# Seven block products in place of eight for twelve of the 22 channel tiles of a down-projection

## The reference

```python
D_MODEL, SEQ, DEPTH, D_FF, CONV_WIDTH = 1024, 512, 2, 2816, 3

def conv_ffn(h, w_up, conv_w, conv_b, w_down):
    gate, val = jnp.split(h @ w_up, 2, axis=-1)
    gate = lax.conv_general_dilated(gate, conv_w[:, None, :], window_strides=(1,),
        padding=((CONV_WIDTH - 1, 0),), dimension_numbers=('NWC', 'WIO', 'NWC'),
        feature_group_count=D_FF) + conv_b
    return (jax.nn.silu(gate) * val) @ w_down
```

## Time and profile before

| what | value |
|---|---|
| median of three runs | 1188.32 us |
| the profiled execution, its own time | 1188.03 us |
| its span | 1186.2 us |
| PE busy | 1174.4 us, 99% |
| granted PE clock, mean | 0.999 of full speed |
| DVE, ACT, POOL busy | 63%, 54%, 57% |
| the two down-projections (from the last up-projection tile to `last_two`) | 498.1 to 596.4 us and 1059.2 to 1157.5 us |

### The profile page before, as it was taken

One profiled execution on the slowest core, in us unless ns is written; L12 is line 12 of the kernel. 1 busy time (PEld: TensorE's weight loads), 2 busy tenths in 40 slices (PEclk: granted clock), 3 DMA queues, 4 the chain that ended last, 5 costly groups with the idle time before them and its releaser, 6 DMA issues.

```text
span 1186.2 us, 21327 instructions
## 1 busy us (share of the span) xinstructions
PE 1174.4 (99%) x7666; PEld 1076.9 (91%) x7670; DVE 746.1 (63%) x1318; ACT 637.3 (54%) x1003; POOL 681.3 (57%) x593
## 2 busy tenths in 40 slices
PE   8999999999999999999999999999999999999997
PEld 7999999889999999988888889978999999998886
DVE  7888777658787777723241375644877787762325
ACT  6665555537665656532343365444766565653334
POOL 2434445326877777666645331611787777766672
PEclk9999999999999999999999999999999999999999
DMA  7232222122332322332223211411233232323221
GB/s 267 100 107 71 90 89 72 36 71 72 115 112 94 110 101 106 125 107 73 104 77 120 106 72 37 142 37 36 75 139 106 98 113 88 113 102 107 92 85 71
DMA packets 17334, 113.83 MB, mean 96 GB/s; under 512 B 1920, under 2 KB 2304, under 8 KB 4608
## 3 DMA queue, kind: packets, MB, share of 16 engines
q1 hardware_dynamic: 16416, 110.20, 26.1%
q10 hardware_dynamic: 864, 2.88, 0.7%
HBM read 110.98 MB, written 2.10 MB: 95 GB/s over the span
## 4 chain that ended last, share of the span: by engine, by line
PE 95%; DVE 2%; ACT 1%; issue 1%; DMA 0%; DVEq 0%; ACTq 0%
PE ps L2118 34%; PE ps L2166 17%; PE ps L1911 9%; PE ps L1768 7%; PE ps L1802 3%; PE ps L1830 3%; PE ps L2299 2%; PE ps L1952 2%; PE ps L1875 2%; PE ps L2279 2%; PE ps L1819 2%; PE ps L1880 1%; PE ps L2203 1%; PE ps L1938 1%; PE ps L1710 1%
## 5 line engine op out<-in xcount | busy, mean ns | idle before, releaser
L350 POOL TENSOR_TENSOR w_lo<-w_raw,w_hi 128x512 fp32r<-128x512 f32 (+2 forms) x169 | 256.9, 1551 | 277.5 <-ACT w_hi L474 221.6
L408 POOL TENSOR_TENSOR w_lo<-w_raw,w_hi 128x512 fp32r<-128x512 f32 x120 | 152.9, 1297 | 85.1 <-ACT w_hi L745 66.6
L474 ACT ACTIVATE w_hi<-w_raw 128x2048 fp32r<-128x2048 f32 (+1 forms) x53 | 95.5, 1801 | 166.4 <-PE ps L2166 129.4
L408 POOL TENSOR_TENSOR s_lo<-s_raw,s_hi 128x512 fp32r<-128x512 f32 x120 | 154.9, 1322 | 0.0
L1454 DVE TENSOR_TENSOR hT_lo<-region,hT_hi 128x2048 fp32r<-128x2048 f32 (+1 forms) x22 | 58.9, 2685 | 138.6 <-ACT hT_hi L821 138.6
L2166 PE MATMUL ps<-w_hi,hT_hi 128*128 128x512 f32 x288 | 112.2, 390 | 0.3
L2166 PE MATMUL ps<-w_hi,hT_lo 128*128 128x512 f32 x288 | 112.0, 389 | 0.0
L2166 PE MATMUL ps<-w_lo,hT_hi 128*128 128x512 f32 x288 | 112.0, 389 | 0.0
L745 ACT ACTIVATE w_hi<-w_raw 128x1536 fp32r<-128x1536 f32 x40 | 59.5, 1488 | 71.8 <-PE ps L2118 71.8
L2118 PE MATMUL ps<-hT_hi,w_hi 128*128 128x256 f32 x320 | 90.8, 284 | 0.0
L2118 PE MATMUL ps<-hT_hi,w_lo 128*128 128x256 f32 x320 | 90.6, 283 | 0.0
(11 more groups left out here) (329 smaller groups left out, 3603.0 us busy)
## 6 DMA issues: line engine op xcount, KB each, us to landing
w_raw<-weights SPq DMA_DIRECT2D x99, 1024.0 KB, 4.8
gain<-gains ACTq DMA_DIRECT2D x4, 512.0 KB, 4.2
x<-x_in SPq DMA_DIRECT2D x3, 512.0 KB, 7.3
out<-region SPq DMA_DIRECT2D x3, 512.0 KB, 2.6
w_raw<-weights SPq DMA_DIRECT2D x2, 384.0 KB, 5.5
w_raw<-weights SPq DMA_DIRECT2D x1, 768.0 KB, 8.5
cst<-consts SPq DMA_DIRECT2D x1, 640.0 KB, 10.3
x<-x_in ACTq DMA_DIRECT2D x1, 512.0 KB, 4.3
```

The lines of the kernel that those rows point to most:

```text
L350: ins = pool.tensor_tensor(w_lo[:, slot, cols], w_raw[:, slot, cols], w_hi[:, slot, cols].bitcast(f32), ALU.subtract)
L408: return pool.tensor_tensor(dst, raw, high.bitcast(f32), ALU.subtract)
L474: sc.activation(w_hi[:, slot, 0:used], w_raw[:, slot, 0:used], ACT.Copy).then_inc(w_hi_ready, 1)
```

## The change

Twelve of the 22 channel tiles are taken as six steps j of two tiles, 2j and 2j+1. In a step the activations are a 2 x 2 of blocks (tokens 0-255 or 256-511 by channel tile 2j or 2j+1: A11, A12, A21, A22) and so are the weights (channel tile by 512 output columns: B11, B12, B21, B22). The products become seven instead of eight, of 6 matmuls each (2 token tiles x 3 passes), with S1 to S4 sums of activation blocks and T1 to T4 sums of weight blocks. They go in three passes over the six steps:

- X units, 0 to 5 after `n1`, one step each: B11, B12 and B22 are loaded (1536 columns). ACT copies B12 to PSUM (`stage_b12`), DVE makes T3 = B22 - B12 and T1 = B12 - B11 (`t1_t3`), ACT the high parts, DVE the low part of T1, POOL those of B11, of S3 and of T3. PE: A11 x B11, S1 x T1, S3 x T3, 18 matmuls a unit.
- Z units, 6 to 8, two steps each, with 2048 columns of plain weights: A12 x B21 and S4 x B22, 24 matmuls a unit. S4 is made by DVE.
- Y units, 9 to 11, two steps each: T3 is copied to PSUM again (`stage_t3`), T2 = T3 + B11 and T4 = T2 - B21 are made by DVE, split by ACT, DVE and POOL. PE: S2 x T2 and A22 x T4, 24 matmuls a unit.

Units 12 to 16 are the other ten channel tiles, 48 matmuls each, as before, with `last_two` on the last two. A layer's down-projection has 17 units in place of 11, and 492 matmuls in place of 528. S1 and S2 are made by POOL during the up-projection (`act_sums`, six pairs). DVE adds the products to `x` in three groups of banks: ten adds after unit 5, four after unit 8 and six after unit 11. The gain of the next norm is loaded by ACT's queue after the X unit 2 and no longer ahead of the down-projection. In `combine_block` of the up-projection the buffer `u2` is now `p1[half]`, in place.

The core of the diff (`down_lows` for the Z and Y units, the Y pass on DVE and the plain units follow the same pattern; a line of "..." is a cut):

```diff
+            for n1, after in ((W_DN0, W_DN1), (W_DN1, W_ALL)):
+                for m in range(n1, n1 + 6):
+                    sp.wait_ge(w_lo_ready, m - 1)
+                    load(m, m % 2, 1536)
+                load_range(n1 + 6, after)
...
+                def act_sums(i):
...
+                    pool.tensor_tensor(s1, s1, a22, ALU.add).then_inc(act_summed[l], 1)
+                    pool.wait_ge(act_summed[l], 2 * i - 1)
+                    pool.tensor_tensor(s2_raw[:, ds(i - 1, 1), :], s1, a11, ALU.subtract).then_inc(act_summed[l], 1)
+                with pool.Fori(1, 7) as i:
+                    pair_lows(i)
+                    act_sums(i)
+                with pool.Fori(7, PAIRS) as i:
...
+            def down_lows(l, n1):
+                for u in X_UNITS:
+                    slot, row = u % 2, 2 * (u % 4) + 1
+                    pool.wait_ge(b11_high[l], u + 1)
+                    low(w_lo[:, slot, 0:512], w_raw[:, slot, 0:512], w_hi[:, slot, 0:512]).then_inc(b11_low[l], 1)
+                    pool.wait_ge(a_highs[l], 2 * u + 2)
+                    low(hT_lo[:, row, 0:256], hT_raw[:, row, 0:256], hT_hi[:, row, 0:256]).then_inc(s3_low[l], 1)
+                    pool.wait_ge(w_hi_ready, n1 + u + 1)
+                    low(w_lo[:, slot, 1024:1536], t3_of(u), w_hi[:, slot, 1024:1536]).then_inc(w_lo_ready, 1)
+                for u in Z_UNITS:
+                    slot = u % 2
+                    pool.wait_ge(w_hi_ready, n1 + u + 1)
+                    for n in range(len(STEPS[u])):
...
+                def stage_b12(u):
+                    loaded(u)
...
+                    sc.activation(ps[:, X_STAGE[u], :], w_raw[:, u % 2, 512:1024], ACT.Copy).then_inc(b12_staged[l], 1)
...
+                def b11_hi(u):
+                    loaded(u)
+                    sc.wait_ge(mm_done, 4 * (n1 + u - 1))
+                    sc.activation(w_hi[:, u % 2, 0:512], w_raw[:, u % 2, 0:512], ACT.Copy).then_inc(b11_high[l], 1)
...
+                def t1_t3_hi(u):
+                    sc.wait_ge(t_sums[l], 2 * u + 2)
+                    sc.activation(w_hi[:, u % 2, 512:1024], ps[:, X_STAGE[u], :], ACT.Copy).then_inc(t_highs[l], 1)
+                    sc.activation(w_hi[:, u % 2, 1024:1536], t3_of(u), ACT.Copy).then_inc(w_hi_ready, 1)
...
+                def x_unit_highs(u):
+                    b11_hi(u)
+                    t1_t3_hi(u)
+                    sum_hi_of(u)
...
+                def y_step_highs(u, n):
...
+                    sc.activation(w_hi[:, slot, 1024 * n:1024 * n + 512], ps[:, T2_BANK[j], :], ACT.Copy).then_inc(t_highs[l], 1)
+                    ins = sc.activation(w_hi[:, slot, 1024 * n + 512:1024 * n + 1024],
+                                        w_lo_raw[:, slot, 1024 * n + 512:1024 * n + 1024], ACT.Copy)
+                    ins.then_inc(t_highs[l], 1)
+                    if j == STEPS[u][-1]:
+                        sc.sem_inc(w_hi_ready, 1)
...
+                for u in range(1, 6):
+                    x_unit_highs(u)
+                    if u == 2:
+                        load_gain()
+                    if u < 5:
+                        stage_b12(u + 1)
+                        a11_s1_hi(u + 1)
+                z_tokens_hi(6)
...
+                    if u < 8:
+                        z_tokens_hi(u + 1)
+                y_tokens_hi(9)
+                for j in range(2):
+                    stage_t3(j)
...
+                stage_t3(2)
+                stage_t3(3)
+                y_step_highs(10, 0)
+                stage_t3(4)
+                y_step_highs(10, 1)
+                stage_t3(5)
+                y_tokens_hi(11)
...
+                def t1_t3(u):
...
+                        ve.wait_ge(mm_done, 4 * n1)
+                    own.link(ve.tensor_tensor(t3_of(u), w_raw[:, slot, 1024:1536], staged, ALU.subtract))
+                    ve.tensor_tensor(staged, staged, w_raw[:, slot, 0:512], ALU.subtract).then_inc(t_sums[l], 2)
+                def t1_low(u):
+                    ve.wait_ge(t_highs[l], u + 1)
+                    ve.tensor_tensor(w_lo[:, u % 2, 512:1024], ps[:, X_STAGE[u], :], w_hi[:, u % 2, 512:1024].bitcast(f32),
...
+                def a11_s1_low(u):
...
+                    ve.wait_ge(a_highs[l], 2 * u + 1)
+                    ve.tensor_tensor(hT_lo[:, row, :], act[:, 2 * u, :], hT_hi[:, row, :].bitcast(f32), ALU.subtract)\
+                      .then_inc(a_lows[l], 1)
...
+                def t2(j):
+                    u, slot, c = step_of(j)
+                    staged = ps[:, T2_BANK[j], :]
+                    ve.wait_ge(w_loaded[slot], 16 * ((n1 + u) // 2 + 1))
+                    ve.wait_ge(t3_staged[l], j + 1)
+                    ve.tensor_tensor(staged, staged, w_raw[:, slot, c:c + 512], ALU.add).then_inc(t_sums[l], 1)
...
+                    ve.wait_ge(mm_done, 4 * (n1 + u - 1))
+                    ve.wait_ge(t_sums[l], 12 + 2 * j + 1)
+                    ve.tensor_tensor(w_lo_raw[:, slot, c + 512:c + 1024], ps[:, T2_BANK[j], :], w_raw[:, slot, c + 512:c + 1024],
+                                     ALU.subtract).then_inc(t_sums[l], 1)
...
+                    if u < 5:
+                        a11_s1_low(u + 1)
+                for u in (6, 7):
...
+                    z_lows(u)
+                after_unit(5, 0)
+                for t in range(2):
+                    add(t, 1, 2 + t)
+                    ins = add(2 + t, 1, 2 + t)
+                ins.then_inc(x_added[l], 1)
+                ve.wait_ge(x_added[l], 1)
+                for t in range(2):
+                    add_both(t, t)
...
+                ins.then_inc(x_added[l], 1)
+                ve.wait_ge(x_added[l], 2)
...
+                ins.then_inc(x_added[l], 1)
+                s4(8)
...
+                for j in range(2):
+                    t2(j)
+                    t4(j)
+                for j in range(2):
+                    t2_low(j)
+                after_unit(8, 2)
+                for t in range(2):
+                    ins = add(t, 0, 6 + t)
...
+                def down_product(row, a0, slot, c, bank, first=False, last=False):
+                    for t in range(2):
+                        for n, (h, w) in enumerate(PASSES):
+                            ins = pe.matmul(ps[:, bank + t, :], h[:, row, a0 + 128 * t:a0 + 128 * t + 128], w[:, slot, c:c + 512],
+                                            start=first and n == 0, stop=last and n == 2)
+                    return ins
...
-                down_tile(0, [(0, four, True, False, every)], False, n1 + 1, 4)
-                pe.wait_ge(act_done[l], 2 * PAIRS)
...
-                          False, n1 + 6, 24)
-                for j in (6, 7, 8):
-                    down_tile(j % 2, [(1, four, False, False, every)], False, n1 + j + 1, 4 * (j + 1))
-                pe.wait_ge(act_lo[l], 40)
-                last_two(n1 + 9, (4, False), (0, False), lambda: pe.wait_ge(act_lo[l], 44))
-
+                for u in X_UNITS:
+                    row, slot = 2 * (u % 4), u % 2
+                    pe.wait_ge(b11_low[l], u + 1)
+                    pe.wait_ge(a_lows[l], u + 1)
+                    down_product(row, 0, slot, 0, 0, u == 0, u == 5)
+                    pe.wait_ge(t_lows[l], u + 1)
+                    down_product(row, 256, slot, 512, 2, u == 0, u == 5)
+                    if u == 0:
+                        pe.wait_ge(act_done[l], 2 * PAIRS)
+                    pe.wait_ge(w_lo_ready, n1 + u + 1)
+                    down_product(row + 1, 0, slot, 1024, 4, u == 0, u == 5).then_inc(mm_done, 4)
+                for u in Z_UNITS:
+                    row, slot = 2 * (u % 4), u % 2
+                    pe.wait_ge(a_lows[l], 6 + 2 * (u - 6) + 2)
+                    pe.wait_ge(step_low[l], u - 6 + 1)
+                    for p, n in ((2, 0), (2, 1), (3, 0), (3, 1)) if u == 6 else ((2, 0), (3, 0), (2, 1), (3, 1)):
+                        if n and p == 2:
+                            pe.wait_ge(w_lo_ready, n1 + u + 1)
+                        if u == 6 and p == 3:
+                            pe.wait_ge(x_added[l], 1)
+                        ins = down_product(row + p - 2, 256 * n, slot, 1024 * n + 512 * (p - 2), 6 if p == 2 else 2,
+                                           u == 6 and n == 0, u == 8 and n == 1)
+                    ins.then_inc(mm_done, 4)
+                for u in Y_UNITS:
+                    row, slot = 2 * (u % 4), u % 2
+                    if u == 9:
+                        pe.wait_ge(x_added[l], 2)
+                    pe.wait_ge(s3_low[l], 6 + u - 9 + 1)
+                    for n, j in enumerate(STEPS[u]):
+                        pe.wait_ge(t_lows[l], 6 + j + 1)
+                        down_product(row, 256 * n, slot, 1024 * n, 0, j == 0, j == 5)
+                        if j == 0:
+                            pe.wait_ge(x_added[l], 4)
+                        if n:
+                            pe.wait_ge(w_lo_ready, n1 + u + 1)
+                        else:
...
```

(6 more changed lines are left out.)

372 lines of the change are left out of this document (282 added, 90 removed).

## The result

The changed kernel takes 1221.95 us (median of four runs, 1220.97 to 1222.99), against 1188.26 us before: a ratio of 1.0284, 95% interval 1.0266 to 1.0302. It is 33.7 us slower; the forecast was 23.3 us slower.

The account below looks back on a forecast made before the run. PE was taken to bound the kernel; 19.8 us lost a layer less 8.18 saved made 11.6 us worse, 23.3 for two layers: 1188.3 + 23.3 = 1211.6 us. The range was 1196 to 1224 us, held at 0.80.

Parts of the forecast that it names:

- the saving: Down-projection on PE: 36 matmuls fewer a layer at 0.2273 us each, 8.18 us a layer, 16.4 us for two.
- its worst prices: Down-projection layout with loads of 4.7 us and slower hand-overs: 23.5 us lost a layer, 1219 us in total.
- start, waiting for `multiply`: Unit 0's third product uses banks 4 and 5 and waits for `multiply`: 1.3 us lost with the hand-over.
- pause before the first plain unit: First plain unit waits for all four pieces of POOL's low parts: 4.0 us lost a layer.
- from unit 13 on PE's 10.9 us a unit hide the rest: Plain units after the first: PE's 10.9 us a unit cover the other engines' work, so no further loss.
- the third rival: Granted clock falls in PE's pauses: nothing to 10.9 us a layer; with 2.7 us, 1217 us in total; chance 0.15.
- The Z term: Z units: 3.2 and 1.2 us of waits at unit 6, 1.7 at unit 8; sum 6.0 us a layer.
- The X term: X units: a slot's loop of 10.7 us for two units against 8.2 of PE; waits of 6.9 us a layer.
- half the gain's collision: X unit 3's load: half of the 1.6 us by which the gain's 512 KB slow a load, landing at 13.7, not 12.9.
- Rival 2: POOL slower throughout, pieces at a mean of 1.80 us: 28 us lost a layer, 1228 us in total; chance 0.09.
- Rival 1: The two-unit load lead holds, slot loop 8.2 us or less: 1178.5 us; chance 0.08, and 0.03 that it just balances.
- The signs: Pauses before X units 3 and 5, Z unit 6, first plain unit; stage about 110 us; POOL over 80% busy in Z, Y.

Follow-up runs that it names:

- The filled pauses: Changed kernel with matmuls into a free PSUM bank in PE's three longest pauses (before Z units 6 and 8 and the first plain unit): 1216.6 us.
- the orders are mended: Changed kernel with high passes first, both X orders, Z unit 8's operands ahead of six adds, and T2's low part earlier in Y units: 1202.0 us.
- the best version: Changed kernel with all those orders together, plus the next norm's gain loaded after the first plain unit's high part, not after X unit 2: 1199.8 us.

## Why the prediction was right, and where its size was off

The direction and the reason held: the saving is taken back, more than twice over, by pauses of PE in which it waits for split and summed operands. 1221.95 us lies in the range; the extra time was 33.7 us and not 23.3. It is above the 1219 us that the layout gave with its worst prices, and inside the range only because this was widened to 26 us lost a layer, for overlaps missed by hand. What was missed, the clock and the short stops, was no overlap, so that the range held is in part luck.

Point by point, for layer 0, forecast against the distances in PE's row:

| part | forecast, us lost | measured |
|---|---|---|
| start, waiting for `multiply` | 1.3 | 1.7 |
| X units | 6.9 | 7.0 |
| Z units | 6.0 | 9.2 |
| Y units | 1.6 | 1.7 |
| pause before the first plain unit | 4.0 | 4.1 |
| slower clock behind that pause | 0 | 2.9 |

(The Z units begin at 531.4 us, after X unit 5, and the Y units at 556.9: 25.5 us for 72 x 0.227 = 16.4. The first plain unit takes 13.8 us from 579.07 on, 10.9 at the full clock.)

- *The saving*, 8.18 us a layer, is right as PE's time: with as many matmuls fewer and the feed of before, the matmuls that remained ran at the same distance. But the step "from unit 13 on PE's 10.9 us a unit hide the rest" and the bound below it were thought of as amounts of work. The run with 36 matmuls fewer showed that the chain through one slot (1.92 + 7.1 us) against one unit of PE is the bound, with 1.6 us in hand.
- *The clock* was the third rival, with 0.15 and a quarter of a unit (2.7 us) behind the plain unit's pause. It came true there with 2.9 us (2.4 in layer 1), and in layer 0 also behind both Z pauses, 2.5 and 2.9 us long, where I had expected none because only the idle of 4 us at the end of the span was in the earlier trace rows. The filled pauses put its price at 5.3 us for the two layers. This rival should have been in the sum: pauses of 3.2 and 4.0 us stood in my own layout.
- *The Z term* was mis-sized: the pauses were 2.7 and 3.0 us (forecast 3.2 and 1.7). The wait for unit 6's other two pieces, forecast 1.2, was 1.6 with the pauses filled, where the Z units lose 7.5 us; in the changed kernel slow starts cover it, and the clock makes the other 1.7 of the 9.2. I gave POOL's first two pieces 0.9 us for the DVE steps beside them; they took 1.28 and 1.71 us, 0.45 more than alone, and the third 1.73.
- *The X term* had nearly the right size for partly the wrong reason. The layout had one loop, the slot's, of 10.7 us (measured 10.92), a wait for it at units 3 and 5 only, and half the gain's collision. In fact every unit lost about the same, the ring of ACT and DVE (5.17 us) would have held it at nearly that pace alone, and the gain fell into a gap.
- *Short stops* were not in the sum: some 4 us a layer (22.2 us lost with the pauses filled, of which 18.1 in pauses). A product whose operand comes at the last moment loses 0.2 to 0.3 us even without a wait to speak of. The up-projection and the old down-projection have none, since their waits were over long before.
- *Rival 2*, POOL slower throughout, did not hold as put: its pieces had a mean of 1.4 us between 530 and 547 us, not 1.8, but the length of POOL's pieces is the largest single cost once the orders are mended (16.3 us, with what hangs on it). *Rival 1*, the lead holds, is out.
- *The signs* held in part. The pauses before Z unit 6 and the first plain unit came, released by POOL's `w_lo`, but no wait in X unit 3 was longer than 0.9 us from start to start where 2 to 3 were forecast, and the one of 1.6 us in X unit 5 stood ahead of its last product; the stage grew to 116.7 and 114.7 us and not 110, and POOL was busy for 80% of the Z units and 68% of the Y units, not over 80% of both.

What stays open: how the remaining 11.5 us of the best version divide among POOL, DVE's steps beside it, the sums and the adds (their place, Z unit 6 above all, is known); and what pause the clock bears.

## What to carry to other kernels

A scheme that trades matmuls for sums pays only where the other engines are far ahead: before shortening PE's unit, add up the chain that one buffer slot goes through (freed, split, low part, ready) and compare it with the time of one unit, not the engines' busy shares with 100%. When an operand comes in parts, let PE begin with the products that need the early part; here that order alone gave back 17 of 34 us, the clock's share included. Look at what an order puts side by side: DVE steps moved next to POOL's took up to three times as long here. And count a pause of PE with what it does to the clock afterwards.

## What the runs showed of the hardware that I had not expected

- Pauses of 2.5 and 2.9 us of PE, after a stage in which it had already stopped briefly at each product, were enough in layer 0 for the granted clock to go to its lower level; the matmuls behind them start 0.43 us apart, for 2 to 4 us. In layer 1 a pause of 2.8 us from start to start before Z unit 8 had no slow start behind it. With other matmuls in the pauses the clock stayed at 1.00.
- A product that is released at the last moment starts its second matmul 0.34 us after its first, not 0.23.
- A 512-wide DVE step with both inputs in SBUF took 0.69 us while POOL was idle and 0.78 to 1.75 us beside its pieces, and a 256-wide one 0.42 and, with the orders changed, up to 1.47 us. POOL's piece took 1.28 us alone and up to 1.8 beside them. Taking some of these DVE steps away gave only 0.7 us all the same. The Trainium skill's rule ("SBUF — State Buffer", SBUF: two separate sides), that a DVE step with two SBUF inputs and a GpSimd step that reads SBUF exclude each other for the whole instruction, agrees with these durations.
